# Weight halves stored element by element in one tile, and moved 64 bytes, in a hybrid decoder trunk

## The chip, the cores and the metric

The kernel runs on one core of one Trainium2 chip. The metric is the device time of one execution in microseconds (us). TensorE (matmuls, and separately their weight loads), VectorE (DVE in the profile), ScalarE (ACT), GpSimd (POOL) and the DMA queues work side by side and wait for one another by semaphores.

## What is computed

Two decoder layers over 512 tokens with a model width of 1024. Layer 0 mixes tokens with a Mamba-2 SSD mixer, layer 1 with differential attention; each is followed by a gated FFN of inner width 2816 with a causal convolution.

```python
for i in range(DEPTH):                       # DEPTH = 2
    hn = rmsnorm(x, norm_mix_pre[i])
    m = mamba2_mixer(hn, ...) if i % 2 == 0 else diff_attention(hn, ...)
    x = x + rmsnorm(m, norm_mix_post[i])
    hn = rmsnorm(x, norm_ffn_pre[i])
    f = conv_ffn(hn, ...)     # (silu(gate) * up) @ w_down, gate and up after the convolution
    x = x + rmsnorm(f, norm_ffn_post[i])
```

Everything is float32. Nearly all the arithmetic lies in the projections: 1024 x 6176 into the mixer and 2048 x 1024 out of it, 1024 x 3072 and 1024 x 1024 for attention, and in each layer 1024 x 5632 up and 2816 x 1024 down.

## The kernel before

**Layout.** Activations stand with features on the 128 partitions and the 512 tokens along the free dimension. A weight matrix is cut into units: one unit holds the weights for 128 output features, as 8 chunks of 128 x 128 (11 in the two down projections, where a unit covers half of the input features). There are eight phases, in this order: MIX (49 units), SOUT (16), UP0 (44), DN0 (16), QKV (24), AOUT (8), UP1 (44), DN1 (16).

**Splitting.** TensorE multiplies in the type float32r. To keep float32 accuracy, each operand is held as two float32r tiles, hi (the value rounded) and lo (the rest). `product` (line 464) makes three matmuls for each chunk: hi weights with hi columns (line 468), hi weights with lo columns (line 469), lo weights with hi columns (line 470). "Columns" here are the moving operand, the tokens: 512 of them, or 256 where a phase is run by halves of the tokens. Each matmul is preceded by its own weight load (LDWEIGHTS) of 128 x 128.

**A unit's way.** SyncE loads the unit's raw float32 weights into one of two slots of `raw` (`load_unit`, line 370). ScalarE copies them, rounded, to the hi tile (`split_hi`, line 416) when TensorE has finished the unit that used the slot before. VectorE subtracts to make the lo tile (`split_lo_dve`, line 431; GpSimd does it in part of QKV, line 422). TensorE waits for `lo_made` and runs the unit; the last matmul raises `unit_done`. The first four units of UP0, QKV and UP1, one unit each of MIX and SOUT and two of AOUT have tiles of their own (`fy`, `fx`, `ay`, `ax`, `own`), so that they can be made ahead. `halves_of` (line 322) says which pair a unit uses.

**Order of the engines' work.** Each engine runs a hand-written list in order. In a mixer group (6 units, the loop body of MIX) TensorE also makes transposes, state matmuls (line 1092) and the matmuls of lines 1080 and 1083, all in plain float32, and VectorE has the convolutions (line 1064), the gating and the six splits. In an FFN up phase VectorE takes two units' results through the convolution and the product of gate and up, with two splits between.

**Where the tiles lie.** Within a partition, the tiles that hold columns (`hn_hi`, `hn_lo`, `y_hi`, `y_lo`, `h_hi`, `h_lo`, `o_hi`, `o_lo`) begin at byte addresses that leave 96 when divided by 128, and each token row in them is 2048 bytes long. The unused tiles `lead_in` and `own_lead` shift the weight tiles:

```python
raw = sb("raw", [P, 2, UW])
sb("lead_in", [P, 56])
w_hi = sb("w_hi", [P, 2, UW], F32R)
w_lo = sb("w_lo", [P, 2, UW], F32R)
sb("lead_out", [P, 72])
```

so that the hi and lo weight tiles leave 96 as well (`w_hi` begins at byte 29,024, `hn_hi` at 86,368). A chunk's 128 weights of one partition lie next to one another, 512 bytes.

Of the kernel before, what the change touches and what calls it, by code (L numbers as in the profile page):

```python
# [18 lines left out]
F32R = mybir.dt.float32r  # L19
# [4 lines left out]
P = 128  # L24
# [3 lines left out]
KC = D // P  # L28
# [9 lines left out]
UW = HU * P  # L38
# [29 lines left out]
def phases():  # L68
    made, prev = [], None
    for units, chunks, width, kind in (  # L70
            (1 + 6 * NG, 1 + 6 * NG, KC * P, "in"), (2 * KC, KC, KC * P, "out"),
            (2 * FC, 2 * FC, KC * P, "in"), (2 * KC, KC, UW, "out"),
            (3 * NH, 3 * NH, KC * P, "in"), (KC, KC, KC * P, "out"),
            (2 * FC, 2 * FC, KC * P, "in"), (2 * KC, KC, UW, "out")):
        prev = Phase(units, chunks, width, kind, prev)
        made.append(prev)
    return made
# [26 lines left out]
def trunk(nc, x_in, w_mix, w_sout, w_up0, w_dn0, w_qkv, w_aout, w_up1, w_dn1, params, lam_in, out):  # L104
    ctx = ExitStack()
    with ctx:
        MIX, SOUT, UP0, DN0, QKV, AOUT, UP1, DN1 = PH = phases()
# [3 lines left out]
        def sb(name, shape, dt=F32, scope=ctx):  # L111
            return scope.enter_context(nc.sbuf_tensor(name, shape, dt))
# [3 lines left out]

        x = sb("x", [P, KC, S])
        raw = sb("raw", [P, 2, UW])
        sb("lead_in", [P, 56])
        w_hi = sb("w_hi", [P, 2, UW], F32R)  # L120
        w_lo = sb("w_lo", [P, 2, UW], F32R)
        sb("lead_out", [P, 72])
        par = sb("par", [P, NPAR])
        lam_v = sb("lam_v", [P, 4 * DH])
        lam_p = sb("lam_p", [P, 2 * DH])
# [27 lines left out]
        with ExitStack() as ssm:  # L153
            with ExitStack() as lap:
                ybuf = sb("ybuf", [P, YC, S], scope=lap)
            y_lo = sb("y_lo", [P, YC, S], F32R, scope=ssm)
            with ExitStack() as lap:
                acs_bc = sb("acs_bc", [P, HG, S], scope=lap)
                sb("early_hi", [P, HG, S], scope=lap)
                xc = sb("xc", [P, 2, S], scope=lap)  # L160
                bT = sb("bT", [P, S], scope=lap)
                cT = sb("cT", [P, S], scope=lap)
                ug_s = sb("ug_s", [P, SSM_T - 1 + S], scope=lap)
                cv_s = sb("cv_s", [P, S], scope=lap)
                btok = sb("btok", [P, NB, P], scope=lap)
                xdd = sb("xdd", [P, NB, HG, HD], scope=lap)
            y_hi = sb("y_hi", [P, YC, S], F32R, scope=ssm)
            sb("gap", [P, 1024], scope=ssm)
            with ExitStack() as lap:
                d_v = sb("d_v", [HS, S], scope=lap)  # L170
                d_e = sb("d_e", [HS, S], scope=lap)
                d_z = sb("d_z", [HS, S], scope=lap)
                t_v, t_w, t_e, t_z, t_p = (sb(n, [P, NB * HS], scope=lap)
                                           for n in ("t_v", "t_w", "t_e", "t_z", "t_p"))
                d_acs = sb("d_acs", [HS, S], scope=lap)
                d_ea = sb("d_ea", [HS, 1], scope=lap)
                last_row = sb("last_row", [P, P], scope=lap)
            xdt = sb("xdt", [P, NB, HG, HD], scope=ssm)
            m_t = sb("m_t", [P, HG, S], scope=ssm)
            cs_t = sb("cs_t", [P, HG, S - P], scope=ssm)  # L180
            cbm = sb("cbm", [P, S], scope=ssm)
            prev = sb("prev", [P, NB - 1, HG, HD], scope=ssm)
            pdec = sb("pdec", [P, HG, HD], scope=ssm)
            yt = sb("yt", [P, 2, S], scope=ssm)
            zs = sb("zs", [P, 2, S], scope=ssm)
            tri = sb("tri", [P, P], scope=ssm)
            dt_tok = sb("dt_tok", [P, NB, HS], scope=ssm)
            nacs = sb("nacs", [P, NB, HS], scope=ssm)
            acs_tok = sb("acs_tok", [P, NB, HS], scope=ssm)
            wdec = sb("wdec", [P, NB, HS], scope=ssm)  # L190
            acs_g = sb("acs_g", [P, NB, HG], scope=ssm)
            ecs_bc = sb("ecs_bc", [P, HG, S], scope=ssm)
            sb("own_lead", [P, 112], scope=ssm)
            own_raw = sb("own_raw", [P, KC * P], scope=ssm)
            own_hi, own_lo = sb("own_hi", [P, KC * P], F32R, scope=ssm), sb("own_lo", [P, KC * P], F32R, scope=ssm)
        with ExitStack() as ffn:
            h_hi = sb("h_hi", [P, FC, S], F32R, scope=ffn)
            h_lo = sb("h_lo", [P, FC, S], F32R, scope=ffn)
            with ExitStack() as lap:
                ug_f = sb("ug_f", [P, FFN_T - 1 + S], scope=lap)  # L200
                cg = sb("cg", [P, S], scope=lap)
                cu = sb("cu", [P, S], scope=lap)
                sg = sb("sg", [P, S], scope=lap)
                hb = sb("hb", [P, S], scope=lap)
            fy_hi, fy_lo = sb("fy_hi", [P, 2, KC * P], F32R, scope=ffn), sb("fy_lo", [P, 2, KC * P], F32R, scope=ffn)
            fx_hi, fx_lo = sb("fx_hi", [P, 2, KC * P], F32R, scope=ffn), sb("fx_lo", [P, 2, KC * P], F32R, scope=ffn)
        with ExitStack() as att:
            o_hi = sb("o_hi", [P, NH, S], F32R, scope=att)
            o_lo = sb("o_lo", [P, NH, S], F32R, scope=att)
            qT = sb("qT", [P, 2, S], scope=att)  # L210
            kT = sb("kT", [P, 2, S], scope=att)
            vT = sb("vT", [P, 2, S], scope=att)
            vtok = sb("vtok", [P, 2, NB, P], scope=att)
            dist_i = sb("dist_i", [P, S], mybir.dt.int32, scope=att)
            dist = sb("dist", [P, S], scope=att)
            sc = sb("sc", [P, 2, 2, S], scope=att)
            pr = sb("pr", [P, 2, 2, S], scope=att)
            at = sb("at", [P, NB, S], scope=att)
            aT = sb("aT", [P, NB, S], scope=att)
            ob = sb("ob", [P, S], scope=att)  # L220
            on = sb("on", [P, S], scope=att)
            with ExitStack() as lap:
                osq = sb("osq", [P, S], scope=lap)
                nmx = sb("nmx", [P, 2, 2], scope=lap)
                den = sb("den", [P, 2, 2], scope=lap)
                cf = sb("cf", [P, 2, 2], scope=lap)
            ay_hi, ay_lo = sb("ay_hi", [P, 2, KC * P], F32R, scope=att), sb("ay_lo", [P, 2, KC * P], F32R, scope=att)
            ax_hi, ax_lo = sb("ax_hi", [P, 2, KC * P], F32R, scope=att), sb("ax_lo", [P, 2, KC * P], F32R, scope=att)

        bank = [ctx.enter_context(nc.psum_tensor(f"bank{i}", [P, S], F32)) for i in range(2)]  # L230
        b_norm = ctx.enter_context(nc.psum_tensor("b_norm", [P, S], F32))
# [84 lines left out]

        WIDE = (UP0, QKV, UP1)

        def slot_of(ph, j):
            return (ph.U0 + j) % 2  # L320

        def halves_of(ph, j, first=False):

            if first and ph in WIDE and j < 4:
                own = ((ax_hi, ax_lo), (ay_hi, ay_lo)) if ph is QKV else ((fx_hi, fx_lo), (fy_hi, fy_lo))
                hi, lo = own[j // 2]
                return hi[:, j % 2, :], lo[:, j % 2, :]
            if first and (ph is MIX and j == 2 or ph is SOUT and j == 6):
                return own_hi[:], own_lo[:]
            if first and ph is AOUT and j in (2, 3):  # L330
                return ax_hi[:, j - 2, 0:ph.width], ax_lo[:, j - 2, 0:ph.width]
            slot = slot_of(ph, j)
            return w_hi[:, slot, 0:ph.width], w_lo[:, slot, 0:ph.width]

        def acc_of(ph, j):
            return bank[(ph.Q0 + j) % 2]
# [14 lines left out]
        def raw_of(ph, j, first=False):  # L351
            if first and ph is MIX and j == 2:
                return own_raw[:]
            return first_raw[:, j, :] if first and ph in WIDE else raw[:, slot_of(ph, j), 0:ph.width]
# [64 lines left out]
        def split_lo(pool, ph, j, rep):  # L419
            hi, lo = halves_of(ph, rep, ph is AOUT and isinstance(j, int))  # L420
            pool.wait_ge(hi_made, ph.U0 + j + 1)
            nc.gpsimd.tensor_tensor(lo, raw[:, slot_of(ph, rep), 0:ph.width], hi.bitcast(F32),
                                    ALU.subtract).then_inc(lo_made, 1)
# [39 lines left out]

        def product(acc, slot, c, hi, lo, first, last, weights=None):

            wh, wl = weights or (w_hi[:, slot, :], w_lo[:, slot, :])
            wh, wl = wh[:, c * P:(c + 1) * P], wl[:, c * P:(c + 1) * P]
            nc.tensor.matmul(acc[:], wh, hi, start=first, stop=False)  # L468
            nc.tensor.matmul(acc[:], wh, lo, start=False, stop=False)  # L469
            return nc.tensor.matmul(acc[:], wl, hi, start=False, stop=last)  # L470
# [1694 lines left out]
```

## Time and profile before

| | |
|---|---|
| median of 3 runs (lowest, highest) | 1436.48 us (1435.9, 1438.88) |
| the profiled execution: its time, its span | 1436.27 us, 1434.5 us |
| TensorE busy, granted clock over the span | 99%, 0.998 |
| VectorE, ScalarE, GpSimd busy | 72%, 43%, 8% |
| DMA engines' mean share, rate | 28.8% for the weights' queue, 99 GB/s |

How to read it: the span runs from the first instruction to the last; what lies around it is 1.8 us. Matmuls overlap in the records: each is listed from its start until its result has drained, so that "busy" says little about pace. The pace is the distance from one start to the next. "PEld" are the weight loads, listed by themselves. A granted clock of 1.00 is 2.4 GHz, 0.50 would be 1.2 GHz.

### The profile page before, as it was taken

What the parts mean: (1) busy time and instruction counts of PE and PEld (TensorE: products, weight loads), DVE (VectorE), ACT (ScalarE), POOL (GpSimd) and SP (SyncE); (2) the same over time, 40 slices, a digit from 0 to 9 for tenths busy, and PEclk for the clock granted to TensorE, in tenths of its full rate; (3) what the DMA queues carried; (4) which work ended last, traced back from release to release, by engine and by line L of the source; (5) the groups of instructions that cost most, each with busy time, mean ns of one, the idle gap of its engine ahead of it and who ended that gap; (6) DMA issues with size and microseconds to landing.
All of it is one profiled execution on the core that took longest, in us unless ns stands there. A gap on an engine that the chain in (4) does not pass through costs nothing.

```text
span 1434.5 us, 21763 instructions
## 1 busy us (share of the span) xinstructions
PE 1417.3 (99%) x7506; PEld 1192.6 (83%) x7506; DVE 1027.8 (72%) x1575; ACT 621.3 (43%) x1019; POOL 112.9 (8%) x85
## 2 busy tenths in 40 slices
PE   8999999999999999999999999999999999999997
PEld 6888888888889888888888977777798888888887
DVE  6998889899437888888623677778588888886123
ACT  6656555557334323323323446556563332323221
POOL 0000000000110000000011032321110000000111
PEclk9999999999999999999999999999999999999999
DMA  4433332432231232323233112121212222233331
GB/s 169 176 137 126 142 125 109 138 140 74 89 132 38 96 102 88 102 91 110 101 101 139 31 59 74 59 74 56 89 63 84 92 102 96 94 105 103 101 101 60
DMA packets 37445, 142.34 MB, mean 99 GB/s; under 512 B 4176, under 2 KB 6352, under 8 KB 35344
## 3 DMA queue, kind: packets, MB, share of 16 engines
q1 hardware_dynamic: 37392, 141.63, 28.8%
q8 instruction: 34, 0.56, 0.2%
q14 instruction: 19, 0.16, 0.0%
HBM read 139.38 MB, written 2.23 MB: 99 GB/s over the span
## 4 chain that ended last, share of the span: by engine, by line
PE 94%; DVE 3%; DMA 1%; ACT 1%; issue 1%; SPq 0%; POOL 0%; POOLq 0%; ACTq 0%
PE bank L468 20%; PE bank L470 20%; PE bank L469 20%; PE b_x L468 7%; PE b_x L470 7%; PE b_x L469 7%; PE b_norm L1647 1%; PE b_norm L489 1%; PE b_y L1080 1%; PE b_y L468 1%; PE b_y L470 1%; PE b_y L469 1%; PE b_cb L1607 1%; DVE hn_lo L823 1%; PE b_x L1092 1%; PE b_y L1597 1%
## 5 line engine op out<-in xcount | busy, mean ns | idle before, releaser
L416 ACT ACTIVATE w_hi<-raw 128x1024 fp32r<-128x1024 f32 (+1 forms) x201 | 222.9, 1109 | 406.3 <-PE bank L470 291.1
L431 DVE TENSOR_TENSOR w_lo<-raw,w_hi 128x1024 fp32r<-128x1024 f32 (+1 forms) x181 | 234.1, 1293 | 229.2 <-ACT w_hi L416 229.1
L468 PE MATMUL bank<-hn_hi,w_hi 128*128 128x512 f32 x848 | 335.9, 396 | 2.9 <-DVE hn_lo L804 1.6
L470 PE MATMUL bank<-hn_hi,w_lo 128*128 128x512 f32 x848 | 330.8, 390 | 0.0
L469 PE MATMUL bank<-hn_lo,w_hi 128*128 128x512 f32 x848 | 330.3, 389 | 0.0
L468 PEld LDWEIGHTS bank<-hn_hi,w_hi 128*128 128x128 f32 x848 | 159.3, 188 | 38.1 <-DVE w_lo L431 3.2
L470 PEld LDWEIGHTS bank<-hn_hi,w_lo 128*128 128x128 f32 x848 | 159.2, 188 | 33.9
L469 PEld LDWEIGHTS bank<-hn_lo,w_hi 128*128 128x128 f32 x848 | 159.4, 188 | 32.1
L468 PE MATMUL bank<-h_hi,w_hi 128*128 128x512 f32 (+1 forms) x352 | 127.9, 363 | 0.0
L470 PE MATMUL bank<-h_hi,w_lo 128*128 128x512 f32 (+1 forms) x352 | 127.6, 362 | 0.0
L469 PE MATMUL bank<-h_lo,w_hi 128*128 128x512 f32 (+1 forms) x352 | 127.6, 362 | 0.0
L468 PE MATMUL b_x<-hn_hi,w_hi 128*128 128x512 f32 x320 | 124.6, 389 | 0.0
L469 PE MATMUL b_x<-hn_lo,w_hi 128*128 128x512 f32 x320 | 124.5, 389 | 0.0
L470 PE MATMUL b_x<-hn_hi,w_lo 128*128 128x512 f32 x320 | 124.5, 389 | 0.0
L1064 DVE SCALAR_TENSOR_TENSOR cv_s<-ug_s,par,cv_s 128x512 f32<-128x512 f32 x96 | 72.0, 750 | 6.9 <-DVE cv_s L1064 0.9
L469 PEld LDWEIGHTS bank<-h_lo,w_hi 128*128 128x128 f32 x352 | 66.4, 189 | 10.3
L470 PEld LDWEIGHTS bank<-h_hi,w_lo 128*128 128x128 f32 x352 | 66.4, 189 | 10.3
L468 PEld LDWEIGHTS bank<-h_hi,w_hi 128*128 128x128 f32 x352 | 66.4, 189 | 10.3
L1498 ACT ACTIVATE sg<-cg 128x512 f32<-128x512 f32 x44 | 27.9, 633 | 104.3 <-DVE cg L1064 104.3
L468 PEld LDWEIGHTS b_x<-hn_hi,w_hi 128*128 128x128 f32 x320 | 60.1, 188 | 13.0 <-issue 0.6
L469 PEld LDWEIGHTS b_x<-hn_lo,w_hi 128*128 128x128 f32 x320 | 60.1, 188 | 12.5
L470 PEld LDWEIGHTS b_x<-hn_hi,w_lo 128*128 128x128 f32 x320 | 60.1, 188 | 12.5
(326 smaller groups left out, 2476.7 us busy)
## 6 DMA issues: line engine op xcount, KB each, us to landing
raw<-w_up SPq DMA_DIRECT2D x80, 512.0 KB, 3.2
raw<-w_mix SPq DMA_DIRECT2D x48, 512.0 KB, 3.3
raw<-w_dn SPq DMA_DIRECT2D x32, 704.0 KB, 4.1
raw<-w_qkv SPq DMA_DIRECT2D x20, 512.0 KB, 3.2
acs_bc<-scratch SPq DMA_DIRECT2D x8, 1024.0 KB, 5.7
ecs_bc<-scratch SPq DMA_DIRECT2D x8, 1024.0 KB, 4.7
raw<-w_sout SPq DMA_DIRECT2D x16, 512.0 KB, 3.2
first_raw<-w_up SPq DMA_DIRECT2D x8, 512.0 KB, 6.4
```

Of the source, the lines that this page charges most:

```text
L416: nc.scalar.activation(halves_of(ph, j if own else rep, own or first and j < 4)[0], raw_of(ph, rep, first and j < 4), ACT.Copy).then_inc(h ...
L431: nc.vector.tensor_tensor(lo, raw_of(ph, rep, first), hi.bitcast(F32), ALU.subtract).then_inc(lo_made, 1)
L468: nc.tensor.matmul(acc[:], wh, hi, start=first, stop=False)
L469: nc.tensor.matmul(acc[:], wh, lo, start=False, stop=False)
L470: return nc.tensor.matmul(acc[:], wl, hi, start=False, stop=last)
L489: last = nc.tensor.matmul(b_norm[:, b:b + 1], squares[:, b * P:(b + 1) * P], mean_col[:, mean:mean + 1], start=True, stop=True)
L823: nc.vector.scalar_tensor_tensor(hn_lo[:, m, tokens(t)], x[:, m, tokens(t)], gain(*GAINS[b][1], m), hn_hi[:, m, tokens(t)].bitcast(F32), A ...
L1064: ins = nc.vector.scalar_tensor_tensor(dst, ug[:, t:t + S], col(wcol + t), dst, ALU.mult, ALU.add)
L1080: last = nc.tensor.matmul(dst, xdt[:, c, hh, :], m_t[:, hh, c * P:(c + 1) * P], start=True, stop=c == 0)
L1092: last = nc.tensor.matmul(b_x[:, c // 2, (c % 2) * 2 * P:(c % 2) * 2 * P + 2 * P], btok[:, c, :], xdd[:, c, :, :].rearrange("p h d -> p (h ...
L1498: nc.scalar.activation(sg[:], cg[:], ACT.Silu).then_inc(gate_ready, 1)
L1597: last = nc.tensor.matmul(scores_in[i % 2][:, t, 0:keys], qT[DH * t:DH * t + DH, b1, i * P:(i + 1) * P], kT[DH * t:DH * t + DH, b1, 0:keys ...
```

## The change

Every pair of a hi and a lo weight tile becomes one tile with a last dimension of 2: element 0 is the hi half, element 1 the lo half. A matmul's weights are then 128 elements with a step of two elements (8 bytes) over 1024 bytes, and the same holds for what ScalarE writes, and for what VectorE and GpSimd read (hi) and write (lo). The tiles before and behind the weights are resized, and 16-element tiles added, so that all weight tiles leave 32 when divided by 128: 64 bytes past the columns, modulo 128 (`w_both` begins at byte 29,088). The raw tile of `own` moves along by 64 bytes; `raw`, `first_raw` and the column tiles stay where they were. Number and order of the instructions, shapes and waits stay as they were.

```diff
         raw = sb("raw", [P, 2, UW])
-        sb("lead_in", [P, 56])
-        w_hi = sb("w_hi", [P, 2, UW], F32R)
-        w_lo = sb("w_lo", [P, 2, UW], F32R)
-        sb("lead_out", [P, 72])
+        sb("lead_in", [P, 72])
+        w_both = sb("w_both", [P, 2, UW, 2], F32R)
+        sb("lead_out", [P, 56])
...
-            sb("own_lead", [P, 112], scope=ssm)
+            sb("own_lead", [P, 128], scope=ssm)
             own_raw = sb("own_raw", [P, KC * P], scope=ssm)
-            own_hi, own_lo = sb("own_hi", [P, KC * P], F32R, scope=ssm), sb("own_lo", [P, KC * P], F32R, scope=ssm)
+            own_both = sb("own_both", [P, KC * P, 2], F32R, scope=ssm)
...
-            fy_hi, fy_lo = sb("fy_hi", [P, 2, KC * P], F32R, scope=ffn), sb("fy_lo", [P, 2, KC * P], F32R, scope=ffn)
-            fx_hi, fx_lo = sb("fx_hi", [P, 2, KC * P], F32R, scope=ffn), sb("fx_lo", [P, 2, KC * P], F32R, scope=ffn)
+            sb("ffn_lead", [P, 16], scope=ffn)
+            fy_both = sb("fy_both", [P, 2, KC * P, 2], F32R, scope=ffn)
+            fx_both = sb("fx_both", [P, 2, KC * P, 2], F32R, scope=ffn)
...
+        def parts(both):
+
+            return both[:, :, 0], both[:, :, 1]
+
...
             slot = slot_of(ph, j)
-            return w_hi[:, slot, 0:ph.width], w_lo[:, slot, 0:ph.width]
+            return parts(w_both[:, slot, 0:ph.width, :])
...
         def product(acc, slot, c, hi, lo, first, last, weights=None):
 
-            wh, wl = weights or (w_hi[:, slot, :], w_lo[:, slot, :])
+            wh, wl = weights or parts(w_both[:, slot, :, :])
             wh, wl = wh[:, c * P:(c + 1) * P], wl[:, c * P:(c + 1) * P]
```

The attention tiles (`ay`, `ax`) change as the FFN's do.

## Rows read from the trace of the kernel before

**Rows 1.** The page: busy time of each engine, share of the span, instructions.
```profile
PE 1417.3 (99%) x7506; PEld 1192.6 (83%) x7506; DVE 1027.8 (72%) x1575; ACT 621.3 (43%) x1019; POOL 112.9 (8%) x85
```

**Rows 2.** The page: shares of the chain that ended last, by engine.
```profile
PE 94%; DVE 3%; DMA 1%; ACT 1%; issue 1%; SPq 0%; POOL 0%; POOLq 0%; ACTq 0%
```

**Rows 3.** Four mixer groups, then FFN units: us, busy us and instructions, clock, DMA share.
```profile
core 0: us, PE busy (x) PEld busy (x) DVE busy (x) ACT busy (x) POOL busy (x), PEclk, DMA share, GB/s
94.28:258.89 164.61, 164.61 (x947) 138.41 (x945) 146.09 (x212) 92.88 (x152) 0.00 (x0) 1.00 0.36 127
500.00:700.00 200.00, 200.00 (x884) 165.62 (x883) 164.72 (x222) 60.98 (x74) 0.00 (x0) 1.00 0.30 99
```

**Rows 4.** Matmuls of line 468 over the whole span: us, busy (x), clock, DMA.
```profile
0.00:1435.00 1435.00, 763.82 (x2064) 1.00 0.29 99
```

**Rows 5.** Line 468, groups of 256 columns, largest and smallest: busy us, mean ns.
```profile
L468 PE MATMUL bank<-h_hi,w_hi 128*128 128x256 f32 x88 | 25.2, 287 | 0.0
...
L468 PE MATMUL b_x<-o_hi,w_hi 128*128 128x256 f32 x16 | 4.6, 287 | 0.0
```

**Rows 6.** TensorE in order of time, 512 columns: start, duration.
```profile
559.75 0.39 PE L468 MATMUL bank<-hn_hi,w_hi 128*128 128x512 f32 x1
559.98 0.39 PE L469 MATMUL bank<-hn_lo,w_hi 128*128 128x512 f32 x1
...
565.19 0.39 PE L468 MATMUL b_x<-hn_hi,w_hi 128*128 128x512 f32 x1
```

**Rows 7.** The same, 256 columns, at the start of the first FFN.
```profile
444.75 0.28 PE L470 MATMUL b_y<-hn_hi,fx_lo 128*128 128x256 f32 x1
...
446.91 0.28 PE L470 MATMUL b_x<-hn_hi,fy_lo 128*128 128x256 f32 x1
```

**Rows 8.** TensorE from state matmuls back to products.
```profile
102.28 1.46 PE L1092 MATMUL b_x<-xdd,btok 128*128 128x256 f32 x6
...
103.80 0.40 PE L469 MATMUL bank<-hn_lo,w_hi 128*128 128x512 f32 x1
104.04 0.40 PE L470 MATMUL bank<-hn_hi,w_lo 128*128 128x512 f32 x1
...
105.88 0.39 PE L469 MATMUL bank<-hn_lo,w_hi 128*128 128x512 f32 x1
```

**Rows 9.** Weight loads by line and shape: count, busy us, mean ns.
```profile
L468 PEld LDWEIGHTS bank<-hn_hi,w_hi 128*128 128x128 f32 x848 | 159.3, 188 | 38.1 <-DVE w_lo L431 3.2 <-issue 2.0 <-DVE hn_lo L804 0.5
...
L1080 PEld LDWEIGHTS b_y<-m_t,xdt 128*64 128x64 f32 x256 | 17.7, 136 | 2.8 <-issue 2.8
```

**Rows 10.** State matmuls, line 1092: duration ns min/median/max.
```profile
L1092 PE MATMUL b_x<-xdd,btok x48: 377/379/483, 61.0 to 350.3; 128*128 128x256 f32 x48
```

**Rows 11.** The splits on VectorE, low halves, by shape: busy us, mean ns.
```profile
L431 DVE TENSOR_TENSOR w_lo<-raw,w_hi 128x1024 fp32r<-128x1024 f32 x149 | 182.0, 1222 | 85.1 <-ACT w_hi L416 85.1
L431 DVE TENSOR_TENSOR w_lo<-raw,w_hi 128x1408 fp32r<-128x1408 f32 x32 | 52.0, 1626 | 144.0 <-ACT w_hi L416 144.0
```

**Rows 12.** The splits on ScalarE, high halves, 1024 elements.
```profile
L416 ACT ACTIVATE w_hi<-raw 128x1024 fp32r<-128x1024 f32 x169 | 178.7, 1057 | 266.0 <-PE bank L470 160.1 <-PE b_x L470 94.5 <-PE b_cb L470 7.8
```

**Rows 13.** What VectorE waited for in the four mixer groups: us, times, longest.
```profile
DVE cs_t L1275 <- ACT cT L1193: 3.4, 4, 0.9
DVE cv_s L1058 <- DVE ug_s L1050: 3.4, 16, 0.3
DVE ug_s L1050 <- ACT xc L1193: 3.1, 4, 0.8
DVE ug_s L1050 <- PE bank L470: 3.0, 4, 0.8
DVE cv_s L1064 <- DVE cv_s L1064: 0.8, 5, 0.2
```

**Rows 14.** The same in the FFN units, the largest.
```profile
DVE w_lo L431 <- ACT w_hi L416: 18.6, 36, 0.9
```

**Rows 15.** What ScalarE's splits waited for, 560 to 660.
```profile
ACT w_hi L416 <- PE bank L470: 26.4, 10, 4.4
```

More of the change, by code:

```diff
@@ L226, in trunk @@
                 cf = sb("cf", [P, 2, 2], scope=lap)
-            ay_hi, ay_lo = sb("ay_hi", [P, 2, KC * P], F32R, scope=att), sb("ay_lo", [P, 2, KC * P], F32R, scope=att)
-            ax_hi, ax_lo = sb("ax_hi", [P, 2, KC * P], F32R, scope=att), sb("ax_lo", [P, 2, KC * P], F32R, scope=att)
+            sb("att_lead", [P, 16], scope=att)
+            ay_both = sb("ay_both", [P, 2, KC * P, 2], F32R, scope=att)
+            ax_both = sb("ax_both", [P, 2, KC * P, 2], F32R, scope=att)
         bank = [ctx.enter_context(nc.psum_tensor(f"bank{i}", [P, S], F32)) for i in range(2)]
@@ L324, in halves_of @@
             if first and ph in WIDE and j < 4:
-                own = ((ax_hi, ax_lo), (ay_hi, ay_lo)) if ph is QKV else ((fx_hi, fx_lo), (fy_hi, fy_lo))
-                hi, lo = own[j // 2]
-                return hi[:, j % 2, :], lo[:, j % 2, :]
+                own = (ax_both, ay_both) if ph is QKV else (fx_both, fy_both)
+                return parts(own[j // 2][:, j % 2, :, :])
             if first and (ph is MIX and j == 2 or ph is SOUT and j == 6):
-                return own_hi[:], own_lo[:]
+                return parts(own_both)
             if first and ph is AOUT and j in (2, 3):
-                return ax_hi[:, j - 2, 0:ph.width], ax_lo[:, j - 2, 0:ph.width]
+                return parts(ax_both[:, j - 2, 0:ph.width, :])
             slot = slot_of(ph, j)
-            return w_hi[:, slot, 0:ph.width], w_lo[:, slot, 0:ph.width]
+            return parts(w_both[:, slot, 0:ph.width, :])
         def acc_of(ph, j):
```

## The prediction

> **What bounds the kernel now.** I read the page first. TensorE is busy 99% of the span, the granted clock is full, VectorE stands at 72%, ScalarE at 43% [rows 1], and the chain that ended last is TensorE for 94% [rows 2]. Nothing that other engines do shortens the run unless TensorE's own pace changes. Then the table of stretches: in four mixer groups and in 200 us of FFN units TensorE has no idle time, VectorE has 89% and 82% [rows 3]. So there are two questions: what sets the pace of a product matmul, and how far behind it VectorE is.
>
> The pace is in the order of time. In steady work 24 matmuls of 512 columns start over 565.19 - 559.75 = 5.44 us, one each 226.7 ns [rows 6]. With 256 columns, 18 start over 446.91 - 444.75 = 2.16 us, one each 120.0 ns [rows 7]. The difference, 106.7 ns for 256 columns, is 0.4167 ns per column, which is the 2.4 GHz level. So 512 columns are 213.3 ns and 256 are 106.7 ns, and both kinds have the same 13.3 ns on top. This excess does not grow with the columns: it is paid once per matmul, and each matmul has one weight load beside it. Line 468 has 2064 matmuls [rows 4]; lines 469 and 470 run as often, 6192 together. Of line 468, 464 have 256 columns (ten groups, the largest and smallest shown) [rows 5], so 1392 of the 6192, and 4800 have 512. The excess is worth 6192 x 13.3 ns = 82.4 us, 5.7% of the run. That is all that a change of the weights' layout can win on TensorE.
>
> Is the excess fixed? After the state matmuls TensorE comes back to products at another rhythm: the first step is 0.24 us, nine steps take 105.88 - 103.80 = 2.08 us, 231.1 ns each, an excess of 17.8 ns; later it is 13.3 again [rows 8]. Same instructions, same tiles, other excess. I read this as a collision of two streams whose cost depends on how they meet, not as a fixed fee.
>
> **What the two streams do.** A load of 128 weights lasts 188 ns and one of 64 weights 136 ns [rows 9]: 52 ns for 64 weights, 0.81 ns each, half the pace of the columns. The columns run through a partition at 4 bytes per 0.417 ns, 9.6 bytes per ns. Packed weights run at 4 bytes per 0.81 ns, 4.9 bytes per ns. The columns therefore overtake the weights by some 490 bytes during a load of 104 ns (128 x 0.81), nearly four times round 128 bytes; if addresses equal modulo 128 get in each other's way, they meet about four times per load. After the change a weight step is 8 bytes: 9.8 bytes per ns, the same as the columns within what these rows resolve. The two then run in step, and the shift of 64 bytes modulo 128 keeps them as far apart as they can be.
>
> **The change part by part.** No instruction, wait or DMA is added, removed or moved. Three costs change.
>
> *TensorE.* The trace has no float32r product with step-2 weights. The nearest row in which both streams run in step is the state matmul of line 1092, plain float32: columns take twice as long there, 213.3 ns for 256, while packed weights keep their pace, so both do 4.8 to 4.9 bytes per ns. Six of them take 1.46 us and the last one lasts 379 ns [rows 8, 10], so one starts each (1.46 - 0.379) / 5 = 0.2162 us: an excess of 2.9 ns instead of 13.3. I take 2.9 as the new excess. The steps become 216.2 and 109.6 ns, a gain of 10.4 ns in each of 6192 matmuls: 64.4 us. The bounds: an excess of nothing gives 82.4 us. On the other side nothing excludes a loss; twice the excess costs 82.4 us (second rival). I am nearer to 2.9, because both the drift argument and a row in step speak for it.
>
> [...]
>
> *VectorE and ScalarE.* VectorE's split takes 1222 ns for 1024 elements and 1626 for 1408 [rows 11], 1.05 ns per element; ScalarE's takes 1057 [rows 12]. Both now touch every other word. No row shows either engine with such a step. From below, no change. From above I bound it at double per element, +1.08 us per split (1024 x 1.05). I take no change: the engines handle one element at a time at 1.05 ns already. ScalarE waits for TensorE before its splits (26.4 us in 100, ten times) [rows 15], so even double would be hidden there.
>
> *What TensorE's faster pace meets.* In four mixer groups VectorE has 146.09 us of work in 164.61 [rows 3]. Its waits on itself and on ScalarE are 3.4 + 3.4 + 3.1 + 0.8 us, and only 3.0 us are a wait on TensorE [rows 13]. Take those 3.0 away and VectorE needs 161.6 us, 40.4 per group. TensorE would need 41.15 - 144 x 0.0104 = 39.65. So VectorE becomes late there: the gain is 0.75 us per group instead of 1.5, over seven groups 5.2 us lost. The late instruction would be the evacuation (line 1050) and the lo split behind it, and TensorE would wait for them. In the FFN units VectorE's wait for the hi split, 18.6 us in 200 [rows 14], is in the end a wait on TensorE; without it VectorE needs 181.4 us, and TensorE would need 200 x 216.2 / 226.7 = 190.7. It stays ahead, with 9.3 us over 37 units, 0.25 us per split. DMA engines are at 30 to 36% [rows 3]; a 5% shorter unit does not change what they set.
>
> **The sum.** 64.4 - 5.2 = 59.2 us. From the profiled execution's own 1436.27 us (span 1434.5, 1.8 around it), 0.2 us under the median shown, that is 1377 us.
>
> **The rivals.**
>
> *A fixed fee (no change).* The 13.3 ns belong to the float32r matmul itself, whatever the weights' addresses. For it: the value is the same for 512 and 256 columns [rows 6, 7], and the row in step is another type with slower columns, which may simply leave room. Against it: 17.8 ns after a restart [rows 8]. Time: 1436.
> [...]
>
> *The price goes by bytes passed (slower).* A load now runs over 1024 bytes instead of 512. If each stretch passed costs the columns a fixed hold-up, the excess doubles to 26.7 ns, and the time is 1436 + 82.4 = 1519 us. The place is the product matmul, and it decides as soon as a step is above 226.7 ns. For it: the excess is paid per load and not per column. Against it: the excess varied with unchanged layout, and in line 1092 a load over the same 512 bytes cost 2.9 ns.
> [...]
>
> *The splits grow (partly eats the gain, or slower).* Above +0.25 us per split VectorE binds the FFN units, and in the mixer every bit counts at once: six splits per group. At double, an FFN unit needs 181.4 / 36.8 + 1.08 = 6.01 us of VectorE against 5.44 now, so 88 units lose 50 us; mixer groups need 46.9 us, seven lose 40. That is 1526 us. Against the kernel of before it loses from +0.13 us per split in the mixer (0.75 / 6) and from +0.51 us in the FFN units (5.44 - 4.93).
>
> *A smaller gain.* The streams are not quite in step, or their start lag puts them on one another for part of the load; half of the excess stays (6.7 ns). 6192 x 6.7 = 41 us less a mixer loss of 1: 1396 to 1433.
>
> **How the numbers follow.** In step and apart as computed: 0.58, 1354 (no excess) to 1392 (excess 5 with the mixer loss). A smaller gain, by streams or by somewhat longer splits: 0.12, 1392 to 1433. No change: 0.10. Slower by either rival: 0.20, 1440 to 1526. The prediction is 1377. The range leaves out the slower cases: 1356 to 1438. A measurement of this kernel tells 0.2% (2.9 us) from no change; faster 0.70, same 0.10, slower 0.20.
>
> **What would show it.** Steps of about 216 ns in the FFN units and about 110 ns at their start, from the first matmul after a restart on. Weight loads that still last 188 ns. Splits of 1222 and 1057 ns. In the mixer groups VectorE without waits on TensorE, and a group of about 40.4 us. The prediction is wrong if the steps stay at 226.7 (fixed fee), lie near 240 (bytes passed), or if `w_lo` splits come out well above 1.22 us and TensorE waits for them.

## The result and the profile after

The changed kernel takes 1452.47 us (1451.07 to 1455.0, 3 runs) against 1436.48: 16.0 us slower, ratio 1.011 with a 95% interval of 1.0081 to 1.0138. The prediction was 1377 us, faster. It was wrong in sign.

The page after gives the same picture as [rows 1]: TensorE busy throughout, the other engines where they were.

```profile
PE 1433.6 (99%) x7506; PEld 1226.0 (85%) x7506; DVE 1029.0 (71%) x1575; ACT 638.4 (44%) x1019; POOL 113.2 (8%) x85
```

The stretches that answer to [rows 3], same columns:

```profile
core 0: us, PE busy (x) PEld busy (x) DVE busy (x) ACT busy (x) POOL busy (x), PEclk, DMA share, GB/s
94.28:258.89 164.61, 164.61 (x941) 141.18 (x940) 145.48 (x213) 94.44 (x151) 0.00 (x0) 1.00 0.36 128
500.00:700.00 200.00, 200.00 (x871) 168.92 (x870) 162.43 (x219) 61.69 (x73) 0.00 (x0) 1.00 0.29 98
```

In 200 us of FFN units there are 871 matmuls instead of 884. A stretch also counts the matmul that was running at its start, so the step is (200 + 0.39) / 871 = 230.1 ns, where before (200 + 0.39) / 884 gives 226.7. In order of time, as [rows 6]:

```profile
559.82 0.39 PE L474 MATMUL bank<-hn_hi,w_both 128*128 128x512 f32 x1
560.04 0.39 PE L472 MATMUL bank<-hn_hi,w_both 128*128 128x512 f32 x1
560.27 0.39 PE L473 MATMUL bank<-hn_lo,w_both 128*128 128x512 f32 x1
560.50 0.39 PE L474 MATMUL bank<-hn_hi,w_both 128*128 128x512 f32 x1
...
565.34 0.39 PE L474 MATMUL bank<-hn_hi,w_both 128*128 128x512 f32 x1
```

24 steps take 565.34 - 559.82 = 5.52 us, 230.0 ns each, an excess of 16.7 ns over the columns' 213.3 instead of 13.3. The steps are not even: three of 0.228 or 0.229 us are followed by one of 0.234, over and over. The 256-column work, as [rows 7]:

```profile
446.60 0.28 PE L473 MATMUL b_y<-hn_lo,fx_both 128*128 128x256 f32 x1
...
448.52 0.28 PE L474 MATMUL b_y<-hn_hi,fx_both 128*128 128x256 f32 x1
```

Here 16 steps take 1.92 us, 120.0 ns each, as before. The weight loads, and the splits as [rows 9, 11, 12]:

```profile
L472 PEld LDWEIGHTS bank<-hn_hi,w_both 128*128 128x128 f32 x848 | 165.1, 195 | 35.1 <-DVE w_both L435 2.9 <-issue 2.0 <-DVE vT L1754 0.7
```

```profile
L435 DVE TENSOR_TENSOR w_both<-raw,w_both 128x1024 fp32r<-128x1024 f32 x149 | 182.2, 1223 | 93.3 <-ACT w_both L420 93.3
```

```profile
L420 ACT ACTIVATE w_both<-raw 128x1024 fp32r<-128x1024 f32 x169 | 193.2, 1143 | 268.6 <-PE bank L474 162.7 <-PE b_x L474 94.7 <-PE b_cb L474 7.9
```

A load lasts 195 ns instead of 188. VectorE's split is unchanged (1223 against 1222 ns); ScalarE's grew from 1057 to 1143 ns, where it waits for TensorE anyway. The sum closes on TensorE alone: 4800 matmuls of 512 columns x 3.33 ns = 16.0 us, the measured difference. That it closes to the tenth is partly luck. The two profiled executions lie 14.8 us apart (spans 1449.3 and 1434.5), and not every phase moved by 3.33 ns. In SOUT the changed kernel runs slower than in the FFN, with its weight tiles at the same 64 bytes past the columns:

```profile
385.12 0.40 PE L472 MATMUL bank<-y_hi,w_both 128*128 128x512 f32 x1
...
387.92 0.40 PE L472 MATMUL b_cb<-y_hi,own_both 128*128 128x512 f32 x1
```

12 steps take 2.80 us, 233.3 ns each.

### The profile page after: what moved, and what is told of

Same layout as the page of the kernel before. It is cut to its first block, busy times and chain, and to the rows that moved or that the text cites. A ratio compares the mean times of both kernels' runs of the same rounds, so it can differ in the third digit from the quotient of the medians.

```text
span 1449.3 us, 21763 instructions
## 1 busy us (share of the span) xinstructions
PE 1433.6 (99%) x7506; PEld 1226.0 (85%) x7506; DVE 1029.0 (71%) x1575; ACT 638.4 (44%) x1019; POOL 113.2 (8%) x85
## 4 chain that ended last, share of the span: by engine, by line
PE 94%; DVE 3%; DMA 1%; ACT 1%; issue 1%; SPq 0%; POOL 0%; POOLq 0%; ACTq 0%
PE bank L472 20%; PE bank L474 20%; PE bank L473 20%; PE b_x L472 7%; PE b_x L474 7%; PE b_x L473 7%; PE b_norm L1651 1%; PE b_norm L493 1%; PE b_y L1084 1%; PE b_y L472 1%; PE b_y L474 1%; PE b_y L473 1%; PE b_cb L1611 1%; DVE hn_lo L827 1%; PE b_x L1096 1%; PE b_y L1601 1%
## 5 line engine op out<-in xcount | busy, mean ns | idle before, releaser
L420 ACT ACTIVATE w_both<-raw 128x1024 fp32r<-128x1024 f32 (+1 forms) x201 | 240.7, 1198 | 409.1 <-PE bank L474 293.8
L435 DVE TENSOR_TENSOR w_both<-raw,w_both 128x1024 fp32r<-128x1024 f32 (+1 forms) x181 | 234.3, 1294 | 240.5 <-ACT w_both L420 240.4
L472 PE MATMUL bank<-hn_hi,w_both 128*128 128x512 f32 x848 | 338.8, 400 | 2.3 <-DVE hn_lo L808 1.5
L474 PE MATMUL bank<-hn_hi,w_both 128*128 128x512 f32 x848 | 333.3, 393 | 0.0
L473 PE MATMUL bank<-hn_lo,w_both 128*128 128x512 f32 x848 | 333.2, 393 | 0.0
L472 PEld LDWEIGHTS bank<-hn_hi,w_both 128*128 128x128 f32 x848 | 165.1, 195 | 35.1 <-DVE w_both L435 2.9
L474 PEld LDWEIGHTS bank<-hn_hi,w_both 128*128 128x128 f32 x848 | 165.0, 195 | 30.5
L473 PEld LDWEIGHTS bank<-hn_lo,w_both 128*128 128x128 f32 x848 | 165.2, 195 | 28.8
L472 PE MATMUL bank<-h_hi,w_both 128*128 128x512 f32 (+1 forms) x352 | 128.7, 366 | 0.0
L473 PE MATMUL bank<-h_lo,w_both 128*128 128x512 f32 (+1 forms) x352 | 128.4, 365 | 0.0
L474 PE MATMUL bank<-h_hi,w_both 128*128 128x512 f32 (+1 forms) x352 | 128.4, 365 | 0.0
L472 PE MATMUL b_x<-hn_hi,w_both 128*128 128x512 f32 x320 | 125.7, 393 | 0.0
L474 PE MATMUL b_x<-hn_hi,w_both 128*128 128x512 f32 x320 | 125.5, 392 | 0.0
L472 PEld LDWEIGHTS bank<-h_hi,w_both 128*128 128x128 f32 x352 | 68.4, 194 | 9.4
L474 PEld LDWEIGHTS bank<-h_hi,w_both 128*128 128x128 f32 x352 | 68.4, 194 | 9.4
```

Of the source, the lines that this page charges most:

```text
L420: nc.scalar.activation(halves_of(ph, j if own else rep, own or first and j < 4)[0], raw_of(ph, rep, first and j < 4), ACT.Copy).then_inc(h ...
L435: nc.vector.tensor_tensor(lo, raw_of(ph, rep, first), hi.bitcast(F32), ALU.subtract).then_inc(lo_made, 1)
```

## Experiments

Five kernels are the trunk with weight tiles in other places. The other six are probes that leave the trunk out: they load columns and weights, run stretches of matmuls in the order of `product` with nothing beside, and write out the input. The places in the expectations are bytes past the columns modulo 128. In the later probes packed weights 128 bytes further gave 232.4 ns and 256 bytes further 226.7 again, so the readings below name the true distance, from the addresses the tiles had. "Packed" weights lie next to one another, "interleaved" ones with a step of two, and "level" means a distance of 0.

### Undo the interleaving, keep the shift

```diff
-        sb("lead_in", [P, 56])
+        sb("lead_in", [P, 72])
         w_hi = sb("w_hi", [P, 2, UW], F32R)
         w_lo = sb("w_lo", [P, 2, UW], F32R)
-        sb("lead_out", [P, 72])
+        sb("lead_out", [P, 56])
...
+            sb("ffn_lead", [P, 16], scope=ffn)
             fy_hi, fy_lo = sb(...)
```

`own_lead` and `att_lead` go along.

> The kernel before with packed hi and lo tiles, but all weight tiles moved to 64 bytes past the columns modulo 128. Theory of place (the excess depends on how far the weights' addresses lie from the columns'): the settled step leaves 226.7 ns for 512 columns, and part or all of the 16 us is here, 1440 to 1460. Theory of step (what costs is that a load passes over 1024 bytes instead of 512): the step stays 226.7 and the time 1436.

Measured: 1460.12 us against 1436.76 (ratio 1.0161, 1.0138 to 1.0183). The FFN stretch, same columns as above:

```profile
500.00:700.00 200.00, 200.00 (x859) 161.15 (x858) 159.31 (x215) 59.67 (x72) 0.00 (x0) 1.00 0.28 97
```

200.39 / 859 = 233.3 ns. So the place alone, with packed weights, costs more than the whole change. The theory of step falls as the only cause.

### Keep the interleaving, move the place

```diff
-        sb("lead_in", [P, 72])
+        sb("lead_in", [P, 56])      # 64 and 80 in the other two
         w_both = sb("w_both", [P, 2, UW, 2], F32R)
-        sb("lead_out", [P, 56])
+        sb("lead_out", [P, 72])     # 64 and 48
```

`own_lead`, `ffn_lead` and `att_lead` go along.

> The changed kernel with its weight tiles moved back to the columns' own remainder modulo 128, so only the interleaving is left. Theory of step: as the changed kernel, 1452 us, steps 229 to 234 ns. Theory of place: streams in step and on one another, so the step must differ clearly from the changed kernel's, above 240 ns if level is the bad place, or below 220 if the true lag of the loads made 64 bytes the bad place.

> The changed kernel with its weight tiles 32 bytes past the columns modulo 128 instead of 64. Theory of step: 1452 us again. Theory of place: another time than at 0 and at 64, by some us or more.

> The changed kernel with its weight tiles 96 bytes past the columns modulo 128. The runs at 0, 32 and 64 gave 1469.8, 1460.6 and 1452.5. If a larger distance goes on helping, below 1452; if the cost comes back round the 128 bytes, between 1455 and 1470. By the theory of step alone 1452 again, which the three places already speak against.

| interleaved, bytes past the columns | time, us | ratio to the kernel before (95%) |
|---|---|---|
| 0 | 1469.75 | 1.0222 (1.02 to 1.0243) |
| 32 | 1460.57 | 1.0163 (1.014 to 1.0185) |
| 64 (the change) | 1452.47 | 1.011 (1.0081 to 1.0138) |
| 96 | 1464.63 | 1.0189 (1.0172 to 1.0206) |

Their FFN stretches, at 0, at 32 and at 96:

```profile
500.00:700.00 200.00, 200.00 (x851) 166.90 (x850) 157.79 (x213) 60.86 (x71) 0.00 (x0) 1.00 0.27 94
```

```profile
500.00:700.00 200.00, 200.00 (x863) 168.45 (x862) 160.38 (x216) 62.18 (x72) 0.00 (x0) 1.00 0.28 97
```

```profile
500.00:700.00 200.00, 200.00 (x859) 168.01 (x858) 159.21 (x215) 62.07 (x72) 0.00 (x0) 1.00 0.28 97
```

That is 235.5, 232.2 and 233.3 ns. Of the four places the change has the best. These are the FFN's steps; at 96 bytes SOUT ran faster than the FFN, at 64 (above) it ran slower:

```profile
399.91 0.39 PE L472 MATMUL bank<-y_hi,w_both 128*128 128x512 f32 x1
...
403.82 0.39 PE L474 MATMUL bank<-y_hi,w_both 128*128 128x512 f32 x1
```

17 steps take 3.91 us, 230.0 ns each. "Above 240 or below 220" was wrong: the effect is real and about half of that size (235.5 is 5.4 above the changed kernel's step, 240 would have been 9.9). With the kernel before and the run before this, the two edits make a square: packed and level 1436, packed and shifted 1460, interleaved and level 1470, both edits together 1452. Neither edit has a price of its own; they interact.

### Probes: is there a free place?

```python
for c in range(KC):
    hi, lo = halves(step, off, c)
    for k, (w, m) in enumerate(((hi, c), (hi, (c + 1) % KC), (lo, c))):
        nc.tensor.matmul(bank[u % 2][0:cols, 0:n], w[:, 0:cols], col[:, m, 0:n], ...)
```

> Not the trunk: only stretches of 96 float32r matmuls in the order of the product (hi, hi, lo) with nothing else running, for weights with step 1, 2 and 4 at 0, 32, 64 and 96 bytes past the columns modulo 128, with 512 and 256 columns, and with loads of 64 weights. Theory of place: among equal steps the start-to-start time changes with the place. Theory of step: 226.7 ns for step 1 everywhere, 229 to 234 for step 2 everywhere, more for step 4. If the excess is a fee of the matmul it is 13.3 ns with 64 weights too; if it is paid by weights read, it is about half there.

Runs of equal matmuls are merged into one line: start, length until the last has drained, count. The step is (length - 0.39) / (count - 1), good to about 0.2 ns. Packed and level, packed at +32, loads with a step of four, and loads of 64 weights:

```profile
39.64 10.59 PE L80 MATMUL bank<-col,s 128*128 128x512 f32 x46
...
61.65 10.66 PE L80 MATMUL bank<-col,s 128*128 128x512 f32 x45
...
209.72 10.50 PE L80 MATMUL bank<-col,s 128*128 128x512 f32 x44
...
329.80 15.57 PE L80 MATMUL bank<-col,s 128*64 128x512 f32 x67
```

226.7, 233.4, 235.1 and 230.0 ns. So the trunk's pace is there without any other engine at work. Half the weights do not halve the excess: it is 16.7 ns with 64 weights, packed and level, where 128 give 13.3. The price is not paid by weights read.

> Not the trunk: stretches of 96 float32r matmuls of 512 columns with nothing else running, at finer places (step 1 at 0, 4, 8, 16, 24, 32, 48, 64, 80, 96, 112, 120, 124 bytes; step 2 at 0 to 112 by 16). If two streams in step and apart could run free of each other, some place of step 2 must come down to about 216 ns. If the excess is a fee with a small part that depends on the place, every place stays between 224 and 240 ns, and step 1 at 0 is a dip by itself.

Packed at 0, at +16, at -4, and interleaved at +64:

```profile
32.71 10.59 PE L82 MATMUL bank<-col,w_a 128*128 128x512 f32 x46
...
88.73 10.43 PE L82 MATMUL bank<-col,w_a 128*128 128x512 f32 x44
...
299.62 10.59 PE L82 MATMUL bank<-col,w_b 128*128 128x512 f32 x46
...
409.83 10.51 PE L82 MATMUL bank<-col,w_d 128*128 128x512 f32 x45
```

226.7, 233.5, 226.7 and 230.0 ns. The other 17 stretches settle between 228.3 and 233.4. Nothing comes near 216: the theory of streams that run free of each other in step and apart falls here.

### Probe: who owns the 13.3 ns?

```python
stretch(lambda w: w_pack[:, 0:P], columns)                                  # the same weights
stretch(packed, lambda m: col[:, 0, :])                                     # the same columns
stretch(lambda w: w_pack[:, w:w + 1].to_broadcast([P, P]), columns)         # one weight, step 0
stretch(packed, lambda m: col_two[:, m // 2, :, m % 2])                     # columns with step 2
stretch(lambda w: w_half[:, w * P:(w + 1) * P], lambda m: col_half[:, m, :])  # bfloat16
stretch(lambda w: w_full[:, w * P:(w + 1) * P], lambda m: x[:, m, :], units=2)  # plain float32
stretch(packed, columns, cols=32)                                           # 32 weights
```

> Not the trunk: stretches of 96 matmuls at place 0, with one thing changed in each: always the same 128 weights; always the same columns; one weight broadcast (step 0); columns with a step of two; bfloat16 with 512 and 256 columns; plain float32; float32r with 384, 256 and 128 columns; 32 weights. If address collisions make the excess, it must vanish when the weights' stream stands still (step 0). If it is a fee of float32r, it stays 13 to 20 ns in every float32r stretch whatever the weights do, and falls to 2 or 3 ns in bfloat16 and plain float32.

The lines in that order:

```profile
61.68 11.04 PE L69 MATMUL bank<-col,w_pack 128*128 128x512 f32 x48
...
83.67 11.04 PE L69 MATMUL bank<-col,w_pack 128*128 128x512 f32 x48
...
105.12 11.66 PE L69 MATMUL bank<-col,w_pack 128*128 128x512 f32 x50
...
128.40 11.96 PE L69 MATMUL bank<-col_two,w_pack 128*128 128x512 f32 x26
...
161.69 5.56 PE L69 MATMUL bank<-col_half,w_half 128*128 128x512 bf16 x25
...
194.82 10.46 PE L69 MATMUL bank<-x,w_full 128*128 128x512 f32 x24
...
281.81 11.98 PE L69 MATMUL bank<-col,w_pack 128*32 128x512 f32 x51
```

How long a single matmul lasted where it was not 0.39 us, and the weight loads:

```profile
L69 PE MATMUL bank<-col_two,w_pack 128*128 128x512 f32 x96 | 43.7, 631 | 0.0
L69 PE MATMUL bank<-x,w_full 128*128 128x512 f32 x96 | 41.4, 592 | 0.0
L69 PE MATMUL bank<-col_half,w_half 128*128 128x512 bf16 x94 | 20.6, 379 | 0.1
```

```profile
L69 PEld LDWEIGHTS bank<-col,w_pack 128*128 128x128 f32 x768 | 131.2, 192 | 47.1 <-ACT w_full L59 26.7 <-issue 0.5
L69 PEld LDWEIGHTS bank<-col_half,w_half 128*128 128x128 bf16 x192 | 18.7, 98 | 13.1 <-issue 0.7
L69 PEld LDWEIGHTS bank<-x,w_full 128*128 128x128 f32 x96 | 18.2, 190 | 22.5 <-issue 22.5
L69 PEld LDWEIGHTS bank<-col,w_pack 128*32 128x32 f32 x96 | 10.4, 109 | 11.5
```

| stretch, 512 columns | step, from the lines above |
|---|---|
| the same weights each time | (11.04 - 0.39) / 47 = 226.6 ns |
| the same columns each time | (11.04 - 0.39) / 47 = 226.6 ns |
| one weight that stands still | (11.66 - 0.39) / 49 = 230.0 ns |
| columns with step two | (11.96 - 0.63) / 25 = 453 ns |
| bfloat16 | (5.56 - 0.38) / 24 = 215.8 ns |
| plain float32, from record to record | (10.46 - 0.59) / 23 = 429.1 ns |
| 32 weights | (11.98 - 0.39) / 50 = 231.8 ns |

bfloat16 is 2.5 ns over 213.3. The plain float32 stretch asks for 48 matmuls and left 96 records of matmuls and 96 of weight loads; from one record to the next it is 2.4 ns over 426.7, twice 213.3.

The probe's expectation asked too much of the weight that stands still: the columns still pass it. By the prediction's own count they would pass it about twice as often as packed weights (some 1000 bytes in a load of 104 ns instead of 490), and loads of 32 weights a quarter as often as loads of 128. The excess is 16.7 and 18.5 ns, where such a count, an estimate from 13.3, gives about 27 and 3. So it does not go by the number of meetings. With the scan of places this decides against the collisions that the prediction reckoned with. At full pace every float32r stretch has an excess of 13.3 ns or more with 512 columns and bfloat16 has 2.5. That bfloat16 loads are shorter (98 ns against 192) does not explain it, since the loads of 32 float32r weights last 109 ns and their excess is 18.5.

Slow columns hide the excess, too. The changed kernel has a short stretch with a granted clock of 0.50, and matmuls at half the pace in it:

```profile
core 0: us, PE busy (x) PEld busy (x) DVE busy (x) ACT busy (x) POOL busy (x), PEclk, DMA share, GB/s
10.20:13.40 3.20, 2.73 (x7) 1.63 (x7) 2.74 (x4) 3.20 (x7) 0.00 (x0) 0.50 1.04 396
```

```profile
12.54 0.63 PE L473 MATMUL bank<-hn_lo,w_both 128*128 128x512 f32 x1
12.96 0.63 PE L474 MATMUL bank<-hn_hi,w_both 128*128 128x512 f32 x1
13.39 0.45 PE L472 MATMUL bank<-hn_hi,w_both 128*128 128x512 f32 x1
```

The two steps take 13.39 - 12.54 = 0.85 us, 425 ns each to the rounding of these rows, with interleaved weights. Each probe begins with 5 to 13 steps of 426 or 427 ns, twice 213.3; a matmul lasts 0.63 us there too, though the clock column reads 1.00. Packed in this probe, and interleaved in a later one (`probe_round`), both float32r and at distance 0:

```profile
27.28 5.32 PE L69 MATMUL bank<-col,w_pack 128*128 128x512 f32 x12
...
15.72 1.91 PE L72 MATMUL bank<-col,w_a 128*128 128x512 f32 x4
```

(5.32 - 0.63) / 11 = 426 and (1.91 - 0.63) / 3 = 427 ns: nothing on top of 426.7, with packed or interleaved weights.

### Probes: what the place does

> Not the trunk: stretches of 96 matmuls. The last probe had two packed places at 226.7 ns (0 and -4 bytes) and 4 bytes at 232. Interleaving puts the lo half 4 bytes behind the hi half, so no place of the tile puts both at 0. If the place of each single load is what counts, then packed hi at 0 with lo at 4 costs like interleaved at 0 (about 231), interleaved with the pair at -4 and 0 comes down towards 226.7, and interleaved hi with hi at 0 is at 226.7. If the step itself costs, the interleaved stretches stay above packed ones at the same places. If the place is relative to the columns, columns at 64 with weights at 64 give 226.7 and with weights at 0 do not; if it is the weights' own address, the other way round. bfloat16 stays at 216 and plain float32 at 2 x 215 wherever the weights lie.

Packed hi at 0 with lo at +4; interleaved at 0 (hi 0, lo 4); interleaved at 0 with hi read for lo too:

```profile
61.21 11.13 PE L78 MATMUL bank<-col,w_a 128*128 128x512 f32 x47
...
105.67 11.70 PE L78 MATMUL bank<-col,w_a 128*128 128x512 f32 x49
...
172.61 10.66 PE L78 MATMUL bank<-col,w_a 128*128 128x512 f32 x45
```

233.5, 235.6 and 233.4 ns. Moving only the lo load by 4 bytes takes the packed kernel's 226.7 away, so each load's own place counts. But the third stretch has every load at 0, as the packed kernel has, and stays 6.7 ns above it: at 0 the step of two costs by itself, and the 4 bytes between the halves are not the reason. At +64 it made no difference either whether lo or hi was read (230.0 ns both). The bfloat16 stretches stayed at 215.8 at both places and also with step 2. The stretch meant for "-4 and 0" lay at +124 and +128; its 231.4 ns answer another question.

> Not the trunk: stretches of 96 float32r matmuls of 512 columns, columns at 0, 32, 64 and 96 bytes modulo 128, each against weights at 0, 32, 64 and 96, first packed, then interleaved; then packed weights at 0, 128, 256, 512 and 1024 bytes further. If the distance modulo 128 decides, the four level pairs of the packed grid are at 226.7 ns and the interleaved grid repeats along its diagonals; the last five stretches are equal. In the last probe columns and weights both at 64 gave 233.3, which speaks against it: then the levels differ by pair, and a period longer than 128 bytes would show in the last five. In every case no stretch falls below 226.7 if 13.3 ns are the fee of float32r.

Packed pairs: columns 0 with weights 0, with +32, with +64; columns 64 with weights 0 (-64); interleaved, columns 0 with +64; packed at +128 and at +256:

```profile
37.65 11.72 PE L75 MATMUL bank<-col,w_a 128*128 128x512 f32 x51
...
60.83 11.36 PE L75 MATMUL bank<-col,w_a 128*128 128x512 f32 x48
...
82.76 11.59 PE L75 MATMUL bank<-col,w_a 128*128 128x512 f32 x49
...
216.69 11.61 PE L75 MATMUL bank<-col_c,w_a 128*128 128x512 f32 x50
...
439.62 10.74 PE L75 MATMUL bank<-col,w_a 128*128 128x512 f32 x46
...
773.82 10.85 PE L75 MATMUL bank<-col,w_a 128*128 128x512 f32 x46
...
795.67 10.59 PE L75 MATMUL bank<-col,w_a 128*128 128x512 f32 x46
```

| step in ns, by weights minus columns | 0 | +32 | +64 | +96 | -64 |
|---|---|---|---|---|---|
| packed | 226.7 | 233.3 | 233.3 | 234.2 | 228.9 |
| interleaved | 233.3 | 232.0 | 230.0 | 233.3 | 233.3 |

All four level packed pairs gave 226.7, and both grids repeat along their diagonals: the distance counts, not either address. But +64 and -64 differ, +128 gives 232.4 and +256 gives 226.7 again, as +512 and +1024 do: for packed weights the period is 256 bytes, not 128. The columns-at-64 stretch of the probe before lay 128 bytes off, which is why its "level" pair gave 233.3.

> Not the trunk: interleaved weights of 512-column products at every 8 bytes round a full 256 bytes past the columns, and at -4, -12, 4 and 12; then packed weights of 256-column products at every 16 bytes round. All earlier probes agree once distances are counted modulo 256 instead of 128. If the interleaved product has no place as good as packed and level, every stretch stays above 226.7 ns and 64 bytes (230.0) is among the lowest; if the 4 bytes between the halves were all that spoilt it, -4 comes to 226.7. For 256 columns the trunk showed 120.0 level and 113.3 at 64 bytes; if 13.3 ns were a fixed fee the lowest would be 120, which that already contradicts, so some places lie between 113 and 118.

Interleaved with 512 columns at +72, packed with 256 columns at +64 (a matmul lasts 0.28 us there):

```profile
117.73 9.59 PE L72 MATMUL bank<-col,w_a 128*128 128x512 f32 x41
...
463.82 9.34 PE L72 MATMUL bank<-col,w_a 128*128 128x256 f32 x81
```

230.0 and 113.3 ns. Of 36 places round the 256 bytes no interleaved one settled below 230.0; five are at 230.0 and the rest lie between 230.9 and 233.5, -4 at 231.1. At +64 this probe settled at 233.3 and the one before at 230.0, at +96 at 230.0 and the one before at 233.3: the same pair can settle at more than one value, as the two SOUT stretches show in the trunk. Each place was tried once here, with 48 matmuls, so 230.0 is the lowest seen and not a proven floor. For 256 columns the best packed place is +64 with 113.3 ns, level gives 120.0.

### A version that follows from it

```diff
             hb = sb("hb", [P, S], scope=lap)
+            sb("ffn_lead", [P, 16], scope=ffn)
             fy_hi, fy_lo = sb(...)
...
+            sb("att_lead", [P, 16], scope=att)
             ay_hi, ay_lo = sb(...)
```

> The kernel before, with only the tiles made ahead for the first units of UP0, QKV, AOUT and UP1 moved 64 bytes past the columns. Those units run with 256 columns, where the packed kernel moved by 64 bytes had a mean step of 118.8 ns against 121.6. About 576 such matmuls, up to 2.8 ns each: 1.6 us faster at most, less 0.3 us for the 48 matmuls of 512 columns that use them in AOUT. If the place mattered only in settled 512-column work, no change.

Measured: 1435.56 us (1435.0 to 1438.26, 11 runs) against 1438.19 (1436.27 to 1439.34, 15 runs) for the kernel before, ratio 0.9987 (0.9978 to 0.9996). At the start of the first FFN:

```profile
443.49 0.28 PE L470 MATMUL b_x<-hn_hi,fy_hi 128*128 128x256 f32 x1
...
446.89 0.28 PE L470 MATMUL b_y<-hn_hi,fx_hi 128*128 128x256 f32 x1
```

30 steps in 3.40 us, 113.3 ns, where [rows 7] has 120.0. So it is faster than the kernel before by about a tenth of a per cent, and than the changed kernel by 1.2%. Not all of the 2.6 us between the medians is the edit's: 9 of the 15 runs before and 4 of the 11 here had a granted clock below 0.998, and the medians of the others, 1436.53 and 1435.56, lie 1.0 us apart, near the 1.3 us expected.

## Why the prediction was wrong

**The bound and the pace.** Right: TensorE sets the run, a product step was 226.7 or 120.0 ns, 13.3 of it excess, and the slower the FFN step of a trunk, the longer it took. Only the packed shifted one, whose place gave the 256 columns 113.3 ns instead of 120.0 in the probe, took 4.5 us less than the interleaved one with the same step of 233.3. VectorE and DMA played no part: TensorE was busy for the whole of each 200 us stretch. Two small terms were put at nothing and were not: ScalarE's split grew by 86 ns (1057 to 1143), hidden as said, and the weight load by 7 ns (188 to 195).

**The step that failed: "I take 2.9 as the new excess".** It rested on reading the 13.3 ns as collisions of the weights' stream with the columns' stream, and on the state matmuls of line 1092 as the row in step. That row is plain float32. It differs from a product in its type and in the pace of its columns, and the runs show that either can account for its small excess: at full pace bfloat16 has 2.5 ns against 13.3 for float32r (the same weights each time; 16.7 with one weight that stands still), and at half pace (426 to 427 ns) float32r has nothing on top. Plain float32 shows 2.4 ns in the controls. Being in step was not the reason: interleaved float32r weights were to be in step, and with loads of 128 weights no place gave less than 16.7. The term measured 16.7 ns instead of 2.9, 4800 x (16.7 - 13.3) = 16 us lost instead of 64 gained.

**"Same instructions, same tiles, other excess."** The observation was sound and was read too far. The excess has two parts: 13.3 ns that every float32r stretch of 512 columns at full pace had, and up to 9 ns more (235.6 against 226.7) that vary with the place, and at one place too (+64 interleaved settled at 230.0 and at 233.3). The waver of [rows 8] fits the second, but no run followed it. From a variable excess I concluded that all of it could go.

**"The shift of 64 bytes modulo 128 keeps them as far apart as they can be."** For packed weights the period is 256 bytes (+128 gave 232.4 ns, +256 gave 226.7). And the kernel before sat level, at the lowest place found for 512 columns (226.7 ns); of the other packed places tried short of 256 bytes only 4 bytes before level was as good, and the rest cost 1.6 to 7.5 ns (228.3 to 234.2). Interleaved weights showed no such place: 230.0 is their lowest in 36. The change gave up the best packed place for the best interleaved one that the trunk runs tried.

**The rivals.** The fixed fee had the better half of the truth and a chance of 0.10; it missed the part that depends on the place. Its time, 1436, was 16 us off. It is not quite fixed either: 256 columns reach 113.3 ns, an excess of 6.7. With everything else equal the place of the weights alone moved the step from 226.7 to 233.3 ns, so for float32r the load is not without effect on the matmul. Bytes passed is refuted: the change costs 3.3 ns, not 13.3, and half the weights cost no less (230.0 ns against 226.7). The splits did not grow on VectorE (1223 ns against 1222). The mixer loss never arose, as TensorE got slower. A row was missing for what the forecast needed, a float32r matmul at full pace beside a slow or still weight stream, and a row of another type and pace was put in its place.

**Open.** Why the place acts with a period of 256 bytes, and what float32r pays the 13.3 ns for, was not found. Nor why one pair settles at different values; that what ran before decides it is a guess. Whether the period is 256 bytes for interleaved weights too was not tried by itself.

## What to carry to other kernels

A row can stand in for a cost only if it shares the type and the pace: here the 2.9 ns of a plain float32 matmul said nothing about float32r, where the same term measured 16.7. When a fee is the same at all sizes but wavers after a restart, split it into a floor and a waver before counting the floor as a gain; a probe of one stretch in the new layout, before the forecast, would have settled it. For float32r products, keep packed weights and columns level modulo 256 bytes with 512 columns (226.7 ns here), try 64 bytes past them with 256 columns (113.3 against 120.0), and measure the step in 20 us of plain matmuls before a kernel is rebuilt.

## What the runs showed of the hardware that I had not expected

- The place of a float32r weight load relative to the columns, modulo 256 bytes, moves the step of 512 columns between 226.7 and 235.6 ns (packed 226.7 to 234.2); bfloat16 stayed at 215.8 at the places tried.
- Reading float32r columns with a step of two elements doubles the step, 453 against 226.7 ns. For the weights it costs 7 ns of load time (195 against 188) and, where every load is level, 6.7 ns of the matmul's step (233.4 against 226.7).
- At half pace the excess of float32r is gone: 426 to 427 ns for 512 columns at the start of the probes, packed or interleaved.
- ScalarE writes 1024 words with a step of two in 1143 ns instead of 1057; VectorE reads and writes so at no cost (1223 against 1222).
